# Identity matmuls in front of six waits of TensorE, in a one-core hybrid encoder step

## The chip, the core and the metric

The kernel runs on one core of one Trainium2 chip. A core has a matrix engine (TensorE, "PE" in the profile, with its weight loads shown apart as "PEld"), a vector engine (DVE), a scalar engine (ACT), GpSimd (POOL), and SyncE (SP), whose queue issues most of the DMAs. Each engine runs its own instruction stream in order; they meet only at semaphores. The metric is the time of one execution in device microseconds; lower is better.

## The reference, cut to what matters

Two layers of an encoder are run for 512 prompt tokens and 32 sample tokens, which the kernel holds side by side as 544 columns. In float32:

```python
# layer 0
qkv_a, z_a, b_a, a_a, q_b, k_b, v_b, f_b = split(rmsnorm(x, g) @ w_in)   # 1024 -> 3596 columns
oa, s_new = gated_delta_rule(qa, ka, va, g, beta, s0)    # chunks of 64 tokens, 4 heads
ob = fox_attention(qb, k_all, v_all, lf_all)             # causal, 4 heads of 128, forget bias
x = x + concat([oa, ob]) @ w_out
# layer 1
q, k, v = split(rmsnorm(x, g) @ w_in)
x = x + swa_attend(q, k, v, valid, sinks) @ w_out        # 16 query heads of 64, window 128
# both layers, after the mixer
x = x + cross_attend(rmsnorm(x, g), mk, mv, wq, wo)      # 4 heads of 128, 256 memory tokens
x = x + square(relu(rmsnorm(x, g) @ w_up)) @ w_down      # 1024 -> 4096 -> 1024
# at the end
y = rmsnorm(x, g_final)                                  # out as rows of tokens
```

The delta rule solves, per chunk of 64 tokens and head, a unit lower triangular system, and then carries a state from chunk to chunk.

## The kernel before, in words

**Projections.** Activations lie as 128 features by 544 tokens. Weights come in panels of 128 x 2048 through two buffers; ACT rounds a panel to its high part, POOL takes the low part, and every product is three matmuls (high by high, high by low, low by high) over two halves of 272 tokens (`block`, the matmul on L744). These are most of TensorE's work.

**Attentions.** There are four of them, all run by the function `attention(name)`: "fox" (17 units), "cross0" and "cross1" (10 units each) and "swa" (40 units). A unit is one block of query tokens for one or two heads. On TensorE a unit has three steps: `scores` (L828) writes the scores into `LP`; `turn` (L851) transposes the probabilities into `MP` banks 0 and 1; `values` (L877, L868 for the sample unit of fox) multiplies them with the values into `MP` bank 2 or 3. Between them DVE takes the maximum (`nm`), ACT the exponential, DVE the normalisation, and ACT copies the transposed probabilities back. The loop over `i` is a software pipeline: at `i` it issues `turn` of unit `i - lag`, `values` of unit `i - lag - 1`, `scores` of unit `i + 1`, and then `also(i)`, a hook that only fox uses. `lag` is 2 for fox and 3 for the others. So the first two score groups are issued at once, and the third one (at `i` = 1) is the first to wait for another engine: for the exponentials of the first unit in the cross attentions, for its maximum in fox and swa. In fox the hook at `i` = 0 waits for ACT's copies of the transposed keys (`turn_act`) and of the sample's forget rows (`rows_act`).

**Ahead of swa** TensorE turns keys and values into rows (L1294, L1295) and then waits until ACT has copied the last of them (`swa_copied`).

**Delta rule.** The steps are written out in one list, `DELTA`, which each engine walks. `gram` builds the decay and gram matrices of a tile, `turns` transposes the start of the inverse, `x..` and `d..` double the solved blocks, `turn_in` fills in transposes of other inputs. Tiles 0 and 1 have 128 tokens (matmuls of 64 x 64), tile `TT` is the sample (32 x 32). `inverse` issues them on L1092, `turn_in` on L1076.

**The last turns.** After the last MLP block DVE scales `x` into `yT`; TensorE waits for it (`y_scaled`), transposes it tile by tile (L1310) and, after the first tile, sums the squares of every token (L1318, ten small matmuls). ACT and DVE scale the turned rows into `y_rows`, and SP sends them out.

In the trace a plain float32 matmul is two MATMUL records, a transpose one.

Of the kernel before, what the change touches and what calls it, by code (L numbers as in the profile page):

```python
# [5 lines left out]
def build_program(nc, t):  # L6
# [29 lines left out]
    NTOK = TT + 1  # L36
# [42 lines left out]
    with ctx:  # L79
# [34 lines left out]
        ident = place("ident", [128, 128])  # L114
# [152 lines left out]
        LP = ctx.enter_context(nc.psum_tensor("LP", [128, 4, 512], f32))  # L267
        MP = ctx.enter_context(nc.psum_tensor("MP", [128, 4, 512], f32))
# [37 lines left out]
        turn_pe, turn_act = sem("turn_pe"), sem("turn_act")  # L306
# [7 lines left out]
        sum_pe, sum_act, sum_dve = sem("sum_pe"), sem("sum_act"), sem("sum_dve")  # L314
# [421 lines left out]
        def _(pe):  # L736
# [76 lines left out]

            XS = (xh, xl)

            def attention(name, also=lambda i: None):
                u0, count = GROUP[name]

                def scores(u):
                    U = UNITS[u]  # L820
                    if u >= 2:

                        pe.wait_ge(ex_ready if UNITS[u - 2]["kind"] == "cross" else nm_ready, u - 1)
                    for g, keys in enumerate(U["keys"]):
                        stacked = U["stack"] > 1
                        rows, at = (slice(NS * g, NS * g + NS), 0) if stacked else (slice(0, U["P"]), g * U["nk"])
                        for kT, n in keys:
                            mm = pe.matmul(LP[rows, score_bank(u, at // 512), at % 512:at % 512 + n], U["q"][g],  # L828
                                           kT, start=True, stop=True, skip_group_check=True)
                            at += n  # L830
                    mm.then_inc(sc_ready, 1)

                def turn(u):
                    U = UNITS[u]
                    P, G_ = U["P"], U["G"]
                    pe.wait_ge(p_ready, u + 1)
                    if U["kind"] == "swa":
                        pe.wait_ge(second_ready, u - GROUP["swa"][0] + 1)
                    if U["stack"] > 1 or u and UNITS[u - 1]["stack"] > 1:

                        pe.wait_ge(pt_ready, u)
                    elif u >= 2:

                        pe.wait_ge(pt_ready, u - 1)
                    for g in range(G_):
                        at = g * U["nk"]
                        for c, (n, _) in enumerate(U["v"]):
                            to = (c * G_ + g) * P
                            bank = (u + to // 512) % 2
                            to %= 512  # L850
                            mm = pe.transpose(MP[0:n, bank, to:to + P], probs_of(u, slice(at, at + n)),  # L851
                                              ident[0:P, 0:P])
                            at += n
                    mm.then_inc(tr_ready, 1)

                def values(u):
                    U = UNITS[u]
                    P, G_, last = U["P"], U["G"], len(U["v"]) - 1
                    pe.wait_ge(pt_ready, u + 1)
                    if u >= 2:  # L860
                        pe.wait_ge(ol_ready, u - 1)
                    if U["stack"] > 1:
                        pe.wait_ge(vpast_in, 16)
                        for g in range(U["stack"]):
                            w = P // U["stack"]
                            for c, (n, v) in enumerate(U["v"]):
                                at = c * P + g * w
                                mm = pe.matmul(MP[:, 2 + u % 2, g * w:g * w + w], v[g], U["PT"][0:n, u % 2, at:at + w],  # L868
                                               start=(g == 0 and c == 0), stop=(c == last), skip_group_check=True)
                        mm.then_inc(o_ready, 1)  # L870
                        return
                    shared = len(U["v"][0][1]) < G_
                    for g in range(1 if shared else G_):
                        w = (G_ if shared else 1) * P
                        for c, (n, v) in enumerate(U["v"]):
                            at = (c * G_ + g) * P
                            mm = pe.matmul(MP[0:U["D"], 2 + u % 2, g * P:g * P + w], v[g],  # L877
                                           U["PT"][0:n, u % 2, at:at + w], start=(c == 0), stop=(c == last),
                                           skip_group_check=True)
                    mm.then_inc(o_ready, 1)  # L880

                lag = 2 + extra_lag(name)
                for i in range(-1, count + lag + 1):
                    if lag <= i < count + lag:
                        turn(u0 + i - lag)
                    if i > lag:
                        values(u0 + i - lag - 1)
                    if i + 1 < count:
                        scores(u0 + i + 1)
                    also(i)  # L890


# [40 lines left out]
            for k in range(KT):  # L933
                for n_, (w, X) in enumerate(((wgh, xh), (wgh, xl), (wgl, xh))):
                    for half, (a, b) in enumerate(TOKENS):
                        mm = pe.matmul(MP[0:GATES, half, 0:HALF], w[:, k, :], X[:, k, a:b],
                                       start=(k == 0 and n_ == 0), stop=(k == KT - 1 and n_ == 2))
# [141 lines left out]
            def inverse(name, j):  # L1079
                _, a, P = TOK[j]  # L1080
# [4 lines left out]
                def dve_at(step_):  # L1085
                    pe.wait_ge(inv_dve[s], count_of(INV_DVE[s], step_, r))
# [10 lines left out]
                if name == "gram":  # L1097
# [18 lines left out]
                        mm = mm_(out, ua[:, H + h, cols_], ua[:, h:H + h + 1:H, cols_])  # L1116
                    mm.then_inc(inv_pe[s], 1)
                elif name == "turns":
                    dve_at("gram")
                    for h, p in each():  # L1120
                        mm = mm_(b1[p, h * C:h * C + C], TmT[s][p, h, :], ident[p, p])
                    mm.then_inc(inv_pe[s], 1)
                elif name[0] == "x":
                    k = sizes.index(int(name[1:]))
                    pe.wait_ge(inv_pool[s], r * len(sizes) + k + 1)
                    if k:
                        dve_at(f"dt{sizes[k - 1]}")
                    else:
                        act_at("turns")
                    for h, p in each():  # L1130
                        mm = mm_(b0[p, h * C:h * C + C], BT[s][p, k % 2, h, :], Tm[s][p, h, :])
                    mm.then_inc(inv_pe[s], 1)
                elif name[0] == "d":
                    k = sizes.index(int(name[1:]))
                    act_at(f"x{sizes[k]}")
                    if k:
                        dve_at(f"dtt{sizes[k - 1]}")
                    if k < len(sizes) - 1:
                        for h, p in each():
                            mm = mm_(b0[p, w + h * C:w + h * C + C], TmT[s][p, h, :], Xm[s][p, h, :])  # L1140
                        mm.then_inc(inv_pe[s], 1)
                    for h, p in each():
                        mm = mm_(b1[p, h * C:h * C + C], Xm[s][p, h, :], TmT[s][p, h, :])
                    mm.then_inc(inv_pe[s], 1)
                else:
                    dve_at(f"dtt{sizes[-1]}")
                    pe.wait_ge(turn_used, max(TURNS.index(("k", j)), TURNS.index(("v", j))) + 1)

                    for h, p in each():
                        mm_(b0[p, 128 * h:128 * h + 128], TmT[s][p, h, :], vbt[j][p, h, :])  # L1150
                    for h in range(H):
                        mm = mm_(b1[:, h * C:h * C + C], kbe[j][parts[0], h, :], TmT[s][parts[0], h, :])
                    mm.then_inc(inv_pe[s], 1)
# [136 lines left out]
            for j, a, P in TOK:  # L1290
                if j >= 2:
                    pe.wait_ge(swa_copied, 1 + j - 1)
                for c in range(2):
                    pe.transpose(MP[0:P, 2 * (j % 2), 128 * c:128 * c + 128], k_c[:, c, a:a + P], ident[:, :])  # L1294
                    mm = pe.transpose(MP[0:P, 2 * (j % 2) + 1, 128 * c:128 * c + 128], v_c[:, c, a:a + P],  # L1295
                                      ident[:, :])
                mm.then_inc(swa_turned, 1)
            pe.wait_ge(swa_copied, 1 + NTOK)
            attention("swa")
            pe.wait_ge(ol_ready, sum(GROUP["swa"]))  # L1300
# [1 line left out]

            for j, a, P in TOK:
                if j == 0:
                    pe.wait_ge(y_scaled, KT)
                if j >= 2:
                    pe.wait_ge(y_left, j - 1)
# [5 lines left out]
                if j == 0:  # L1313
# [3 lines left out]
                    for i, at, Q in TOK:  # L1317
                        mm = pe.matmul(MP[0:Q, 0, i:i + 1], acc[:, at:at + Q], ones[:, 0:1], start=True, stop=True,  # L1318
                                       skip_group_check=True)
# [1022 lines left out]
```

## Time and profile before

| what | us |
|---|---|
| median of 3 runs | 1736.03 |
| lowest, highest | 1728.38, 1737.19 |
| the profiled execution | 1740.99 |
| its span, first to last instruction | 1739.3 |
| TensorE busy | 1649.8 (95%) |
| DVE, ACT, POOL busy | 748.7, 602.7, 533.2 |

The mean granted clock of TensorE in the profiled execution is 0.963 of full speed. The row `PEclk` of the page gives it slice by slice: 9 tenths or more nearly everywhere, 8 in five of the forty slices. Windows of the trace give it for any stretch: 1.00 is the upper level (2.4 GHz), 0.50 the lower (1.2 GHz), and a value between them is a stretch with some of both.

### The profile page before, as it was taken

How to read it: one execution, taken by the hardware profiler on the slowest of the kernel's cores; microseconds unless marked ns; L12 is line 12 of the kernel's file. 1: busy time of each engine (PE TensorE's matmuls, PEld its weight loads, DVE VectorE, ACT ScalarE, POOL GpSimd, SP SyncE). 2: the span in 40 equal slices, each digit the busy share in tenths (PEclk: the TensorE clock that was granted, in tenths of full speed). 3: DMA queues.
4: the chain of work that ended last, by engine and by line, in shares of the span. 5: the costliest groups of instructions: out<-in, count | busy, mean ns of one | idle time of the engine just before them, and what ended most of it. 6: DMA issues, size and time to landing. Idle time of an engine off the chain costs nothing.

```text
span 1739.3 us, 31388 instructions
## 1 busy us (share of the span) xinstructions
PE 1649.8 (95%) x13305; PEld 1561.1 (90%) x13305; DVE 748.7 (43%) x1338; ACT 602.7 (35%) x1105; POOL 533.2 (31%) x192
## 2 busy tenths in 40 slices
PE   6999988999989999989989998999889999999998
PEld 6999967888978999989989995559878999999998
DVE  4592165435746422313224425765755322222245
ACT  5132264224434422313123216773443413222232
POOL 4633202121441333433433341003522344343341
PEclk9998999999999999999989998899999999999998
DMA  5232111004340233232212331001410332322321
GB/s 152 74 96 74 51 51 56 2 2 133 103 131 16 68 97 97 74 98 73 94 57 94 98 127 56 1 1 61 153 55 25 98 97 74 98 76 93 96 72 52
DMA packets 123051, 131.67 MB, mean 76 GB/s; under 512 B 6285, under 2 KB 115122, under 8 KB 122930
## 3 DMA queue, kind: packets, MB, share of 16 engines
q1 hardware_dynamic: 116064, 123.27, 21.9%
q10 hardware_dynamic: 6866, 6.63, 1.2%
q8 instruction: 95, 1.56, 0.4%
q14 instruction: 26, 0.21, 0.0%
HBM read 122.44 MB, written 7.45 MB: 75 GB/s over the span
## 4 chain that ended last, share of the span: by engine, by line
PE 87%; DVE 7%; ACT 3%; issue 2%; DMA 0%; ACTq 0%; DVEq 0%
PE LP L744 69%; PE LP L828 3%; PE MP L877 3%; PE LP L1092 3%; PE MP L851 2%; DVE acc L1851 1%; DVE xl L1858 1%; DVE probs L1919 1%; PE MP L1186 1%; PE MP L1172 1%; DVE nm L1924 1%; PE MP L1180 0%; DMA stage<-in_w_in_ab 0%; DVE nm L1896 0%; PE LP L1310 0%
## 5 line engine op out<-in xcount | busy, mean ns | idle before, releaser
L638 POOL TENSOR_TENSOR wl<-stage,wh 128x2048 fp32r<-128x2048 f32 x107 | 493.3, 4610 | 1013.2 <-ACT wh L1342 1013.1
L744 PE MATMUL LP<-xh,wh 128*128 128x272 f32 x2176 | 462.2, 294 | 22.9 <-issue 9.7
L744 PE MATMUL LP<-xh,wl 128*128 128x272 f32 x2176 | 455.8, 291 | 0.0
L744 PE MATMUL LP<-xl,wh 128*128 128x272 f32 x2176 | 455.1, 291 | 0.0
L744 PEld LDWEIGHTS LP<-xh,wh 128*128 128x128 f32 x2176 | 348.2, 192 | 26.5 <-DVE xl L1858 8.8
L1342 ACT CAST wh<-stage 128x2048 fp32r<-128x2048 f32 x107 | 203.7, 1905 | 460.2 <-PE LP L744 459.4
L744 PEld LDWEIGHTS LP<-xl,wh 128*128 128x128 f32 x2176 | 348.3, 192 | 2.2 <-issue 2.2
L744 PEld LDWEIGHTS LP<-xh,wl 128*128 128x128 f32 x2176 | 345.5, 192 | 0.0
L744 PE MATMUL LP<-hh,wh 128*128 128x272 f32 x1024 | 211.5, 288 | 0.0
L744 PE MATMUL LP<-hh,wl 128*128 128x272 f32 x1024 | 210.9, 288 | 0.0
L744 PE MATMUL LP<-hl,wh 128*128 128x272 f32 x1024 | 210.6, 287 | 0.0
L2242 DVE TENSOR_TENSOR hsq<-rel 128x544 f32<-128x544 f32 x64 | 70.5, 1101 | 283.7 <-ACT rel L1762 277.2
L744 PEld LDWEIGHTS LP<-hl,wh 128*128 128x128 f32 x1024 | 160.2, 188 | 0.0
L744 PEld LDWEIGHTS LP<-hh,wl 128*128 128x128 f32 x1024 | 159.6, 189 | 0.0
L744 PEld LDWEIGHTS LP<-hh,wh 128*128 128x128 f32 x1024 | 159.5, 188 | 0.0
L2257 DVE TENSOR_TENSOR dtmp<-LP,rstd 128x544 f32<-128x544 f32 x64 | 46.3, 724 | 234.8 <-PE LP L744 234.8
L1762 ACT ACTIVATE rel<-LP 128x544 f32<-128x544 f32 x64 | 40.1, 626 | 253.3 <-PE LP L744 253.3
L1851 DVE TENSOR_TENSOR acc<-acc,sq 128x544 f32<-128x544 f32 x49 | 81.9, 1671 | 23.4 <-ACT sq L1367 23.4
L1858 DVE SCALAR_TENSOR_TENSOR xl<-x,cols,xh 128x544 fp32r<-128x544 f32 x48 | 78.6, 1648 | 24.0 <-ACT xh L1372 23.8
L1367 ACT ACTIVATE sq<-x 128x544 f32<-128x544 f32 x56 | 36.8, 658 | 138.2 <-DVE x L1872 75.0
L721 POOL TENSOR_TENSOR BT<-LT,level 128x256 f32<-128x256 f32 (+1 forms) x24 | 18.1, 768 | 141.4 <-DVE LT L2142 113.0
L851 PEld LDWEIGHTS MP<-ident,probs 128*128 128x128 f32 (+2 forms) x269 | 31.1, 150 | 29.5 <-DVE probs L1950 16.4
(374 smaller groups left out, 1811.1 us busy)
## 6 DMA issues: line engine op xcount, KB each, us to landing
stage<-in_w_up SPq DMA_DIRECT2D x32, 1024.0 KB, 5.4
stage<-in_w_down SPq DMA_DIRECT2D x32, 1024.0 KB, 5.2
stage<-in_w_in_ab SPq DMA_DIRECT2D x13, 1024.0 KB, 5.2
stage<-in_w_xkv SPq DMA_DIRECT2D x8, 1024.0 KB, 5.3
stage<-in_w_in_c SPq DMA_DIRECT2D x6, 1024.0 KB, 5.0
stage<-in_w_out_ab SPq DMA_DIRECT2D x4, 1024.0 KB, 9.9
stage<-in_w_xq SPq DMA_DIRECT2D x4, 1024.0 KB, 5.5
stage<-in_w_xo SPq DMA_DIRECT2D x4, 1024.0 KB, 5.9
```

Of the source, the lines that this page charges most:

```text
L638: pool.tensor_tensor(wl[s][:, :], stage[s][:, :], wh[s][:, :].bitcast(f32), ALU.subtract).then_inc(w_lo, 1)
L744: mm = pe.matmul(LP[:, 2 * slot + half, 0:b - a], weights, X[part][:, k, a:b], start=(first and n_ == 0), stop=(last and n_ == 2), skip_gr ...
L828: mm = pe.matmul(LP[rows, score_bank(u, at // 512), at % 512:at % 512 + n], U["q"][g], kT, start=True, stop=True, skip_group_check=True)
L851: mm = pe.transpose(MP[0:n, bank, to:to + P], probs_of(u, slice(at, at + n)), ident[0:P, 0:P])
L877: mm = pe.matmul(MP[0:U["D"], 2 + u % 2, g * P:g * P + w], v[g], U["PT"][0:n, u % 2, at:at + w], start=(c == 0), stop=(c == last), skip_gr ...
L1092: return pe.matmul(out, lhsT, rhs, start=start, stop=stop, skip_group_check=True)
L1342: act.copy(wh[s][:, :], stage[s][:, :]).then_inc(w_hi, 1)
L1762: act.activation(rel[:, k % 2, :].rearrange("p (a n) -> p a n", a=2), LP[:, 2 * (k % 2):2 * (k % 2) + 2, 0:HALF], ACT.Relu).then_inc(relu_ ...
L1851: dve.tensor_tensor(acc[:, :], acc[:, :], sq[:, k % 2, :], ALU.add).then_inc(sq_used, 1)
L1858: dve.scalar_tensor_tensor(out=xl[:, k, :], in0=x[:, k, :], scalar=gain(n_, k), in1=xh[:, k, :].bitcast(f32), op0=ALU.mult, op1=ALU.subtra ...
L2242: dve.tensor_tensor(hsq[:, k % 2, :], rel[:, k % 2, :], rel[:, k % 2, :], ALU.mult).then_inc(hsq_ready, 1)
L2257: dve.tensor_tensor(two(dtmp[:, k % 2, :]), banks(k), two(rstd[:, :]), ALU.mult).then_inc(drained, 1)
```

## The change: what it does

A helper `keep_busy(count, bank)` issues `count` matmuls of the 128 x 128 float32 identity with itself into a PSUM bank. Nobody reads what they write, and they signal no semaphore. It is called

- in every attention, at `i` = 0, after the scores of the second unit and before the hook: 8 matmuls in fox and swa, 16 in each cross attention, into `MP` bank 2 (in fox behind an added wait for the eleventh copy of turned rows, which frees the bank);
- in the delta rule, ahead of the first `turns` step (tile 0 only, it runs once): 6, into `MP` bank 1, behind an added wait for ACT's reading of the gate sums there;
- between the turned keys and values and the wait ahead of swa: 6, into `LP` bank 3;
- ahead of the wait for `yT` at the end: 8, into `MP` bank 2.

That is 68 matmuls in an execution. No other engine's stream changes.

```diff
--- before.py
+++ after.py
@@ -813,6 +813,11 @@
 
             XS = (xh, xl)
 
+            def keep_busy(count, bank):
+
+                for _ in range(count):
+                    pe.matmul(bank[:, 0:128], ident[:, :], ident[:, :], start=True, stop=True, skip_group_check=True)
+
             def attention(name, also=lambda i: None):
                 u0, count = GROUP[name]
 
@@ -887,6 +892,10 @@
                         values(u0 + i - lag - 1)
                     if i + 1 < count:
                         scores(u0 + i + 1)
+                    if i == 0:
+                        if name == "fox":
+                            pe.wait_ge(turn_act, 2 * NTOK + 1)
+                        keep_busy({"fox": 8, "swa": 8}.get(name, 16), MP[:, 2, :])
                     also(i)
 
 
@@ -1116,6 +1125,9 @@
                         mm = mm_(out, ua[:, H + h, cols_], ua[:, h:H + h + 1:H, cols_])
                     mm.then_inc(inv_pe[s], 1)
                 elif name == "turns":
+                    if j == 0:
+                        pe.wait_ge(sum_act, 1)
+                        keep_busy(6, MP[:, 1, :])
                     dve_at("gram")
                     for h, p in each():
                         mm = mm_(b1[p, h * C:h * C + C], TmT[s][p, h, :], ident[p, p])
@@ -1295,6 +1307,7 @@
                     mm = pe.transpose(MP[0:P, 2 * (j % 2) + 1, 128 * c:128 * c + 128], v_c[:, c, a:a + P],
                                       ident[:, :])
                 mm.then_inc(swa_turned, 1)
+            keep_busy(6, LP[:, 3, :])
             pe.wait_ge(swa_copied, 1 + NTOK)
             attention("swa")
             pe.wait_ge(ol_ready, sum(GROUP["swa"]))
@@ -1302,6 +1315,7 @@
 
             for j, a, P in TOK:
                 if j == 0:
+                    keep_busy(8, MP[:, 2, :])
                     pe.wait_ge(y_scaled, KT)
                 if j >= 2:
                     pe.wait_ge(y_left, j - 1)
```

Where they stand, by TensorE's stream. The rows give the line, the operation, the output and the inputs, the shape, and the semaphores waited for; the new helper stands ahead of the later code, so that the lines of the kernel after are higher (L828 is L833 there, L1092 is L1101).

Start of cross0, before: the last projection matmul, the scores of units 0 and 1, of units 2 and 3, and the first transposes.

```order
L744 MATMUL LP<-xh,wl_57 128x272 x2
L828 MATMUL LP<-kvT,q_x 128x256 [waits nm_ready,drained,rstd_ready]
L828 MATMUL LP<-kvT,q_x 128x256
L828 MATMUL LP<-kvT,q_x 128x256 [waits nm_ready]
L828 MATMUL LP<-kvT,q_x 128x256
L828 MATMUL LP<-kvT,q_x 128x256 [waits ex_ready]
L828 MATMUL LP<-kvT,q_x 128x256
L828 MATMUL LP<-kvT,q_x 128x256 [waits ex_ready]
L828 MATMUL LP<-kvT,q_x 128x256
```

The same place after.

```order
L744 MATMUL LP<-xh,wl_57 128x272 x2
L833 MATMUL LP<-kvT,q_x 128x256 [waits nm_ready,drained,rstd_ready]
L833 MATMUL LP<-kvT,q_x 128x256
L833 MATMUL LP<-kvT,q_x 128x256 [waits nm_ready]
L833 MATMUL LP<-kvT,q_x 128x256
L819 MATMUL MP<-ident 128x128 x16
L833 MATMUL LP<-kvT,q_x 128x256 [waits ex_ready]
L833 MATMUL LP<-kvT,q_x 128x256
L833 MATMUL LP<-kvT,q_x 128x256 [waits ex_ready]
L833 MATMUL LP<-kvT,q_x 128x256
```

The sixteen stand between the second unit's scores and the first wait for `ex_ready`, with no wait of their own.

Start of swa after: the last turned rows (`k_c`, `v_c`), the six, the scores of units 0 and 1, the eight, the scores of units 2 and 3. Before, the rows of L819 are not there and the others are the same.

```order
L1306 MATMUL MP<-ident,k_c 32x128
L1307 MATMUL MP<-ident,v_c 32x128
L819 MATMUL LP<-ident 128x128 x6
L833 MATMUL LP<-k_c,q_c 128x128 [waits ex_ready,swa_copied]
L833 MATMUL LP<-k_c,q_c 128x128
L833 MATMUL LP<-k_c,q_c 128x256 [waits ex_ready]
L833 MATMUL LP<-k_c,q_c 128x256
L819 MATMUL MP<-ident 128x128 x8
L833 MATMUL LP<-k_c,q_c 128x256 [waits nm_ready]
L833 MATMUL LP<-k_c,q_c 128x256
```

Both groups come ahead of a wait: of `swa_copied` the first, of `nm_ready` the second.

The delta rule after: the last matmuls of `gram` for the sample tile, the transposes of tile 0's keys, the six, and `turns` of tiles 0, 1 and the sample (`TmT_128`, `TmT_129`, `TmT_130`).

```order
L1101 MATMUL MP<-ua 32x2x32 x4
L1085 MATMUL MP<-ident,ua 128x128 x4
L819 MATMUL MP<-ident 128x128 [waits sum_act]
L819 MATMUL MP<-ident 128x128 x5
L1101 MATMUL LP<-ident,TmT_128 64x64 [waits inv_dve0]
L1101 MATMUL LP<-ident,TmT_128 64x64 x7
L1101 MATMUL LP<-ident,TmT_129 64x64 [waits inv_dve1]
L1101 MATMUL LP<-ident,TmT_129 64x64 x7
L1101 MATMUL MP<-ident,TmT_130 32x32 [waits inv_dve2]
L1101 MATMUL MP<-ident,TmT_130 32x32 x3
```

The six stand ahead of the turns of tile 0, two waits earlier than the wait for the sample's `TmT`.

## Rows read from the trace of the kernel before

**Rows 1.** The page: TensorE's busy time, its granted clock by slice.

```profile
PE 1649.8 (95%) x13305; PEld 1561.1 (90%) x13305; DVE 748.7 (43%) x1338; ACT 602.7 (35%) x1105; POOL 533.2 (31%) x192
...
PEclk9998999999999999999989998899999999999998
```

**Rows 2.** Windows: stretch, length, busy of five engines, clock, DMA share, GB/s.

```profile
222.74:225.52 2.78, 0.00 (x0) 0.00 (x1) 1.00 (x5) 1.10 (x5) 0.00 (x0) 1.00 1.05 405
...
237.94:244.77 6.83, 6.83 (x25) 5.81 (x26) 2.18 (x8) 3.44 (x8) 0.00 (x0) 0.50 0.00 0
...
285.73:292.56 6.83, 6.20 (x80) 5.15 (x82) 3.46 (x6) 1.16 (x4) 1.85 (x3) 0.50 0.01 2
514.41:517.84 3.43, 0.00 (x1) 0.00 (x0) 3.43 (x1) 0.00 (x0) 3.43 (x1) 1.00 0.00 0
517.84:524.66 6.82, 5.44 (x14) 3.58 (x15) 3.87 (x13) 3.66 (x14) 0.25 (x1) 0.50 0.47 154
...
1057.14:1074.21 17.07, 16.05 (x47) 9.26 (x47) 10.27 (x45) 11.15 (x42) 0.00 (x0) 0.50 0.14 49
...
1282.43:1289.25 6.82, 4.30 (x12) 3.22 (x12) 4.07 (x9) 2.95 (x12) 1.39 (x1) 0.50 0.49 154
...
1726.15:1732.98 6.83, 6.83 (x34) 6.54 (x33) 2.25 (x3) 2.76 (x7) 0.00 (x0) 0.50 0.32 131
1732.98:1734.27 1.29, 1.27 (x12) 0.91 (x10) 0.75 (x1) 0.69 (x1) 0.00 (x0) 1.00 0.84 321
```

**Rows 3.** Chain of waits, cross0: start, length, what; eight 128x128 float32 records.

```profile
525.87 0.89 PE MP L877 x8
```

**Rows 4.** Timeline of TensorE, both cross attentions: start, length, what, idle before.

```profile
512.44 1.97 PE L828 MATMUL LP<-kvT,q_x 128*128 128x256 f32 x8 [0.86 <-issue]
519.22 3.78 PE L828 MATMUL LP<-kvT,q_x 128*128 128x256 f32 x8 [4.81 <-ACT probs L1395]
...
1284.95 3.78 PE L828 MATMUL LP<-kvT,q_x 128*128 128x256 f32 x8 [4.81 <-ACT probs L1395]
```

**Rows 5.** Timeline, delta rule: turns of tiles 0, 1; DVE; turns of TT; three doublings.

```profile
281.65 1.47 PE L1092 MATMUL LP<-ident,TmT 64*64 64x64 f32 x32
...
283.32 1.79 DVE L2146 TENSOR_TENSOR TmT<-chunk_ident,TmT 32x128 f32<-32x128 f32 x1
...
285.16 0.43 PE L1092 MATMUL MP<-ident,TmT 32*32 32x32 f32 x8 [2.04 <-DVE TmT L2146]
...
287.40 1.97 PE L1092 MATMUL LP<-Tm,BT 64*64 64x64 f32 x32
...
294.81 1.15 PE L1092 MATMUL LP<-Tm,BT 64*64 64x64 f32 x32
...
300.01 1.15 PE L1092 MATMUL LP<-Tm,BT 64*64 64x64 f32 x32
```

**Rows 6.** Timeline of TensorE, swa: first scores, then the sample unit's in three groups.

```profile
1054.20 1.57 PE L828 MATMUL LP<-k_c,q_c 64*128 64x128 f32 x8 [1.63 <-ACT v_cn L1806]
1056.14 1.13 PE L828 MATMUL LP<-k_c,q_c 64*128 64x256 f32 x4 [0.36 <-DVE nm L1929]
...
1078.04 0.40 PE L828 MATMUL LP<-kcT,q_c 64*32 64x128 f32 x2
...
1090.03 0.40 PE L828 MATMUL LP<-kcT,q_c 64*32 64x128 f32 x2
...
1104.80 0.40 PE L828 MATMUL LP<-kcT,q_c 64*32 64x128 f32 x2
```

**Rows 7.** Window in swa, between the second and third of those groups.

```profile
1091.28:1098.10 6.82, 6.61 (x19) 3.85 (x20) 4.02 (x20) 5.75 (x23) 0.00 (x0) 0.50 0.00 0
```

**Rows 8.** Timeline of TensorE, last turns: the first tile, then the sums of squares.

```profile
1725.27 1.17 PE L1310 MATMUL LP<-ident,yT 128*128 128x128 f32 x8 [2.12 <-DVE yT L2270]
1726.23 2.01 PE L1318 MATMUL MP<-ones,acc 128*128 128x1 f32 x10
```

**Rows 9.** Window in the last turns.

```profile
1731.00:1732.00 1.00, 1.00 (x7) 1.00 (x6) 0.02 (x1) 0.03 (x1) 0.00 (x0) 0.50 1.00 406
```

## The prediction, made before the changed kernel was run

> **What bounds the kernel now.** I read the page first. TensorE is busy for 95% of the span, and the clock row stays at 8 or 9 tenths in every slice [rows 1]. So the projections fill the kernel; the change touches none of them and can act only in the short stages where TensorE waits. Then I cut the stages into windows, with the clock beside the busy time. TensorE's clock has two levels here, 1.00 and 0.50 of full speed (2.4 and 1.2 GHz). In both cross attentions, in the delta rule and in the last turns it falls after the engine has stood still for a few microseconds, and it comes back after TensorE has worked for a while at the lower level [rows 2]. Last I read the timeline around each fall, to see which engine is waited for there.
>
> The change removes nothing. It fills waits of TensorE with matmuls whose result is thrown away. It gains only if three things hold: the clock would have fallen, it now does not, and TensorE is what the stage waits for in the stretch saved.
>
> **Price of the filler.** Eight records of the 128x128 float32 matmul take 0.89 us in a row at full clock [rows 3], 0.111 us each, and a matmul is two records: 0.22 us. Sixteen are 3.6 us, eight 1.8 us, six 1.3 us; all 68 are 15 us at full clock. No other engine does more. What of the 15 us lies in front of work that could have started is the cost.
>
> **Price of the lower clock.** A stretch that is TensorE's alone costs half its length. Two repeated patterns show what it costs in the real stages. In swa the same five units take 11.99 us from group to group at full clock (1078.04 to 1090.03) and 14.77 us when 6.82 us of them lie at the lower clock (1090.03 to 1104.80) [rows 6, 7]: 2.78 / 6.82 = 0.41 us per microsecond. In the delta rule one doubling takes 5.20 us at full clock (294.81 to 300.01) and 7.41 us (287.40 to 294.81) when 5.16 us of it are low [rows 5, 2]: 0.43. I use 0.42.
>
> **Cross attentions.** TensorE stands still for 4.81 us in each, waiting for ACT's exponentials of the first unit [rows 4]; DVE is the late one behind that, busy all through the wait [rows 2]. The sixteen matmuls take 3.6 of the 4.81 us and end 1.2 us before TensorE is needed, so they delay nothing. If that cover shrank below 3.6 us, they would cost the difference. With them TensorE is idle for 1.2 us, and I expect no fall. What is saved is 5.44 and 4.30 us of busy time at the lower clock [rows 2]: 9.74 x 0.42 = 4.1 us. I take off 0.4 us, because right after the gap the third and fourth units' scores (3.78 us for eight records, low) come out at the pace at which DVE can take them. Term 3.7 us, bounds 2.8 (DVE decides until the first transposes) and 4.9 (all of it at one half).
>
> **Fox.** Idle 2.78 us and no fall: the clock is 1.00 in the gap and falls only at 237.94, 15 us later [rows 2]. There, between 234 and 240, TensorE runs narrow matmuls of the sample unit, which the filler does not touch. The eight (1.8 us) fit into 2.78, and the added wait for ACT's eleventh copy is over by then: that copy precedes the key copies, which ACT makes ahead of what ends the gap. In this execution the term is 0. A fall after a gap of 2.04 us in the delta rule and none after 2.78 us here tells me that falls are not tied to the length of the gap alone, and that other executions may have one here. Term 0.5 us, bounds -0.3 and +1.7 (four low microseconds avoided).
>
> **Delta rule.** The six stand ahead of the turns of tiles 0 and 1, which today wait for nothing. They push these back by 1.3 us, but behind them TensorE stands still for 2.04 us, since DVE takes 1.79 us for the sample's `TmT` [rows 5], which the change leaves where it is. So the push is absorbed. If that slow DVE step ran in some 0.3 us instead, the six would cost the whole 1.3 us. The clock was low from 285.73 to 292.56, 6.83 us, 6.20 busy [rows 2]. Avoiding all of it is worth 6.20 x 0.42 = 2.6 us. But the filler lies ahead of busy work and not in the gap: the 2.04 us shrink to 0.7 us, a short matmul follows, then a further wait, so the clock may fall a little later all the same. I take somewhat under half: 1.2 us, bounds -1.3 and +2.6.
>
> **Swa.** The first six fill 1.3 of a gap of 1.63 us [rows 6] and cost nothing. The eight stand ahead of the third unit's scores, which waited for 0.36 us only [rows 6]: 1.8 - 0.36 = 1.4 us too late. The fourth unit's scores wait for DVE again and run at full clock in place of low, so about 0.6 us reach DVE. The low stretch is long, 1057.14 to 1074.21, 17.07 us [rows 2], but the filler ends before its first third: at its start the scores are 64 rows deep and wait on DVE, and the stage later falls to the lower clock with no idle time of a microsecond before it, as at 1091.28 [rows 7]. So I expect the fall to come later, not to stay away: some 3 us of TensorE's work less at the lower clock, 1.3 us, less 0.6. Term 0.6 us, bounds -1.4 (the fall where it was) and +6.4 (16.05 busy microseconds x 0.42, less 0.4).
>
> **Last turns.** The eight (1.8 us) fit into 2.12 us of waiting [rows 8]. Low from 1726.15 to 1732.98 [rows 2]. At full clock the ten sums of squares (2.01 us) are between 1.0 and 2.01 us, which brings the first evicted tile up to 1.0 us forward; the later transposes gain more, but the output DMAs then run at 406 GB/s with a share of 1.00 [rows 9], so little of it reaches the end. Term 1.0 us, bounds 0 and 2.7.
>
> A rule of the skill speaks against this term. The Trainium skill, page "TensorE: Matmul & The Clock Gate", Part 4 (PE-mode transpose), says that transposes do not count as activity for the clock as matmuls do. By that rule the clock falls in the last turns anyway, soon after the filler, the term is 0 and the sum 6.0 us. The trace disagrees: after the sums of squares at 1728.2 TensorE ran transposes only, and the clock rose during them, at 1732.98 [rows 2].
>
> **Sum.** 3.7 + 0.5 + 1.2 + 0.6 + 1.0 = 7.0 us. Against the profiled execution's own 1740.99 us that is 1734.0. That execution is 5.0 us above the median of the three runs, 1736.03, so the forecast for the median is 1729.0 us. With all lower bounds the sum is -0.2 us, with all upper ones 18.3 us; both ends at once are unlikely.
>
> **The rivals.**
>
> *The clock stays up through the start of swa too.* For it: 1054.20 to 1057 had only short waits, and the fall comes at their end [rows 6, 2], so 14 matmuls more may carry the engine over the fill of the pipeline. Against it: stretches without fillers in the same stage fall as well [rows 7]. It would replace swa's 0.6 by some 5.5 us, and the delta rule's 1.2 by 2.6: 13.3 us, 1722.7 us.
>
> *The fillers do not hold the clock.* The fall only moves behind them, into the same work. For it: the lower level in fox came without an idle gap, from narrow matmuls alone [rows 2]. Against it: the fall in cross0 follows 3.43 us of complete idleness [rows 2]. Then half the cross term stays, the delta rule and swa give 0 or less: 1.9 - 0.3 + 0.5 = 2.1 us, 1733.9 us.
>
> *Slower.* Place: the eight in swa. They delay the third unit by 1.4 us, and the fall of the clock moves from the fill of the pipeline, where DVE decides, into the part where TensorE decides. If two more low stretches of the length of rows 7 come up in swa (2 x 2.78 us), the 1.4 us reach the end, the delta rule's 1.3 us are uncovered, and the rest brings 0, that is 8.3 us slower, 1744.3 us. It decides only if the cross attentions, whose fillers lie wholly in idle time, give nothing at the same time; with their 3.7 us it is 4.6 us slower, 1740.6 us. Against it: twice 4.81 us of idle time [rows 4] are too plain.
>
> **How the numbers follow.** Forecast (1729.0) 0.52; clock up in swa too (1722.7) 0.22; not held (1733.9) 0.18; slower (1740 and above) 0.08. A measurement of this kernel can tell about 0.5% from no change, 8.7 us: faster means below 1727.3, slower above 1744.7. The three runs before spread over 8.8 us by themselves, so a median of three may lie 3 us off. The forecast case is then below 1727.3 in a third of its cases (0.17), the swa case in nearly all (0.20): 0.37. The slower case gets there in half of its cases, with 0.02 from the spread: 0.06. Within 0.5%: 0.57. The range of 8 in 10 goes from 1719.5 to 1738.0; it leaves out the far end of the swa case and most of the slower one. The likeliest case alone spans 1724 to 1734.
>
> **What would show it.** In the profile after: no row at 0.50 in the first 6 us after the scores of the second unit in either cross attention, and a wait of about 1.2 us instead of 4.81 before the third unit's scores; the first eight score records after it in about 2 us and not 3.78. In the delta rule the wait for `TmT` near 0.7 us. In swa the third unit's scores right behind the filler and a low stretch that starts later than 3 us after the first scores. At the end 1.00 during the ten sums. The forecast is wrong if the clock is at 0.50 in a cross attention, if its third unit comes more than 4.9 us after the second, or if swa, first scores to projection, changes by more than 4 us.

## The result, and the profile after

The kernel after takes 1711.22 us (median of 4 runs, 1710.72 to 1726.52), the kernel before 1736.61 us (4 runs, 1728.38 to 1739.32). The ratio is 0.9862 with a 95% interval of 0.9824 to 0.9899: 1.4% faster, some 25 us, where I had forecast 7. The time lies outside my range of 1719.5 to 1738.0. Here and below, means and medians leave out the few executions that are more than 1.5% above the fastest of the same kernel.

The first rows of the page of the kernel after, which answer to [rows 1]:

```profile
span 1709.0 us, 31660 instructions
...
PE 1635.6 (96%) x13441; PEld 1554.6 (91%) x13441; DVE 747.8 (44%) x1338; ACT 602.7 (35%) x1105; POOL 533.2 (31%) x192
...
PEclk9998999998999999999999999899999999999999
```

TensorE issues 136 more matmul records (68 fillers of two records) and is busy for 14 us less: the others ran at a higher clock. The span is 30.3 us shorter, 1739.3 to 1709.0; that is more than the medians differ by, since the profiled execution before is a long one (1740.99). To find where, I cut both traces at the same instructions. In brackets stands how much of the stage lay at the lower clock.

| stage, on TensorE | before, us | after, us | difference |
|---|---|---|---|
| forget sums to fox | 77.63 (9.7) | 77.90 (10.2) | +0.27 |
| fox, from its third scores | 46.50 (6.8) | 46.50 (6.8) | 0.00 |
| delta rule, from `turns` of the sample | 109.77 (13.7) | 107.01 (7.2) | -2.76 |
| cross0, from its third scores | 24.55 (5.4) | 22.75 (0.0) | -1.80 |
| **cross0's output, first MLP, in_c** | **505.35 (20.5)** | **487.72 (0.0)** | **-17.63** |
| swa | 115.61 (41.0) | 111.21 (23.9) | -4.40 |
| out1, memory, xq1 | 108.36 (3.4) | 106.89 (0.0) | -1.47 |
| cross1, from its third scores | 24.02 (4.3) | 22.75 (0.0) | -1.27 |
| second MLP | 416.30 (3.4) | 415.93 (0.0) | -0.37 |
| last turns | 14.00 (9.7) | 12.69 (2.3) | -1.31 |

(At the very start the kernel after is 0.6 us late, by its first inputs.) More than half of the gain comes from a stage with no filler in it. The two windows of that stage, of the kernel before and of the kernel after:

```profile
543.77:1049.12 505.35, 490.86 (x3848) 488.94 (x3848) 160.03 (x188) 137.42 (x140) 179.50 (x39) 0.98 0.27 87
```

```profile
539.93:1027.65 487.72, 482.89 (x3849) 481.59 (x3849) 160.04 (x188) 137.52 (x140) 179.64 (x39) 1.00 0.28 89
```

Idle time of TensorE (length less the first busy number) goes from 14.49 to 4.83 us, 9.7 us less, and its busy time falls by 8.0 us for the same instructions, which is the clock. What ended the idle time stands in the waits of TensorE between 560 and 1040 us, before and after (us in total, times, longest):

```profile
PE LP L744 <- issue: 9.7, 4, 4.1
PE LP L744 <- DVE xl L1858: 2.1, 2, 1.8
PE LP L744 <- DVEq L1874: 1.9, 1, 1.9
```

```profile
PE LP L744 <- DVE xl L1872: 2.1, 2, 1.8
PE LP L744 <- DVEq L1888: 1.9, 1, 1.9
```

The first row is gone: 9.7 us in which TensorE waited for no engine. Its four places in the timeline before:

```profile
770.94 0.81 PE L744 MATMUL LP<-xh,wh 128*128 128x272 f32 x2 [3.65 <-issue]
...
773.73 0.39 PE L744 MATMUL LP<-xh,wh 128*128 128x272 f32 x1 [0.85 <-issue]
...
874.56 0.82 PE L744 MATMUL LP<-xh,wh 128*128 128x272 f32 x2 [4.07 <-issue]
...
877.63 0.39 PE L744 MATMUL LP<-xh,wh 128*128 128x272 f32 x1 [1.12 <-issue]
```

They are 104 us apart, one turn of the first MLP's loop, at its start. (The loop has three turns, so the program jumps back twice.) The clock falls in each of the two long waits:

```profile
770.42:777.25 6.83, 5.46 (x23) 5.37 (x24) 0.00 (x0) 0.00 (x0) 3.38 (x1) 0.50 0.32 90
...
872.82:883.06 10.24, 7.38 (x32) 7.29 (x33) 0.00 (x0) 0.00 (x0) 4.21 (x1) 0.50 0.33 105
```

These are 17.1 of the 20.5 us at the lower clock. The other 3.4 us, at 575.86, come long before the first jump; profiles without a filler in cross0 have them even where no jump waits, and there they cost some 0.3 us (below). The DMA view names what else happens there: the queue that brings instructions. Between 770 and 1020 us, before and after (packets, MB, share):

```profile
q8 instruction: 19, 0.31, 0.6%
```

```profile
q8 instruction: 3, 0.05, 0.1%
```

A packet is 16 KB. Between 755 and 955 us the contrast is plainer: 17 packets of this queue before, and after none at all, only one of another queue:

```profile
q8 instruction: 17, 0.28, 0.7%
```

```profile
q14 instruction: 1, 0.01, 0.0%
```

The view does not name the engine that the packets are for, but their spacing points to TensorE: inside a turn of the kernel before they come 13 to 18 us apart, and 128 matmuls with their 128 weight loads, 256 instructions, take 16.0 us at the 0.125 us of one matmul. So before, TensorE's code of the loop is fetched again in every turn, and the jump back waits for it. After, it is not. The Trainium skill, page "Runtime: NRT & Kernel Launch", section "Instruction fetch mechanics", says that code comes in blocks of 16 KB or 256 instructions, and that TensorE's instruction memory has 128 KB, 2048 instructions, which is eight blocks. It also says that a taken jump waits for a fetch when its target is outside the present window; it calls that window two pages, which is the memory that it gives for the other engines. The packet size agrees. A window of two blocks for TensorE does not: after, the loop jumps back over more than six blocks without a packet. By that page, an estimate: the loop has 768 matmuls and as many weight loads, six blocks and some more, so it lies in seven blocks or in eight depending on where it begins. How many blocks TensorE holds, and why one place is fetched anew and another not, no run here shows.

Where the fillers stand, the picture is as forecast. Cross0 after: the sixteen matmuls, and the third and fourth scores, at full clock.

```profile
512.18 3.73 PE L819 MATMUL MP<-ident 128*128 128x128 f32 x32
517.18 2.04 PE L833 MATMUL LP<-kvT,q_x 128*128 128x256 f32 x8 [1.27 <-ACT probs L1409]
```

The wait is 1.27 us in place of 4.81, and the eight score records take 2.04 us in place of 3.78 [rows 4]. In the delta rule the six, and the wait for the sample's `TmT`, 1.03 us against 2.04 [rows 5] (I had forecast 0.7):

```profile
282.34 1.50 PE L819 MATMUL MP<-ident 128*128 128x128 f32 x12
...
285.95 0.43 PE L1101 MATMUL MP<-ident,TmT 32*32 32x32 f32 x8 [1.03 <-DVE TmT L2160]
```

And in the last turns the eight, the first tile and the ten sums, 1.18 us against 2.01 [rows 8]:

```profile
1694.03 1.95 PE L819 MATMUL MP<-ident 128*128 128x128 f32 x16
...
1696.30 1.09 PE L1324 MATMUL LP<-ident,yT 128*128 128x128 f32 x8 [0.33 <-DVE yT L2284]
...
1697.23 1.18 PE L1332 MATMUL MP<-ones,acc 128*128 128x1 f32 x10
```

### The profile page after: what moved, and what is told of

It reads as the page before. It is cut to its first block, busy times and chain, and to the rows that moved or that the text cites. A ratio compares the mean times of both kernels' runs of the same rounds, so it can differ in the third digit from the quotient of the medians.

```text
span 1709.0 us, 31660 instructions
## 1 busy us (share of the span) xinstructions
PE 1635.6 (96%) x13441; PEld 1554.6 (91%) x13441; DVE 747.8 (44%) x1338; ACT 602.7 (35%) x1105; POOL 533.2 (31%) x192
## 4 chain that ended last, share of the span: by engine, by line
issue 42%; PE 42%; POOL 8%; DVE 4%; ACT 2%; DMA 1%; ACTq 0%; POOLq 0%; DVEq 0%
PE LP L744 34%; POOL wl L638 8%; PE LP L1101 2%; DVE acc L1865 1%; PE MP L882 1%; PE LP L833 1%; DVE xl L1872 1%; DMA stage<-in_w_in_ab 1%; PE MP L856 0%; DVE conv_sum L2022 0%; DMA stage<-in_w_xkv 0%; PE MP L945 0%; ACT sq L1381 0%; PE MP L873 0%; PE MP L1101 0%
## 5 line engine op out<-in xcount | busy, mean ns | idle before, releaser
L744 PE MATMUL LP<-xh,wh 128*128 128x272 f32 x2176 | 457.3, 291 | 15.3 <-DVE xl L1872 8.1
L744 PEld LDWEIGHTS LP<-xh,wh 128*128 128x128 f32 x2176 | 344.5, 190 | 20.4 <-DVE xl L1872 10.7
L744 PEld LDWEIGHTS LP<-xl,wh 128*128 128x128 f32 x2176 | 344.2, 190 | 0.0
L744 PEld LDWEIGHTS LP<-xh,wl 128*128 128x128 f32 x2176 | 341.8, 190 | 0.0
```

Of the source, the lines that this page charges most:

```text
L744: mm = pe.matmul(LP[:, 2 * slot + half, 0:b - a], weights, X[part][:, k, a:b], start=(first and n_ == 0), stop=(last and n_ == 2), skip_gr ...
```

## The experiments

Two theories. *Place*: most of the gain is that the added instructions shift the first MLP's loop in TensorE's code, so that it is not fetched anew. *Clock*: the gain is what the fillers do to the clock. The runs vary shift and activity apart from each other. A small matmul of a 32 x 32 corner has the same four instructions as a filler (two matmuls, two weight loads) and takes about 0.07 us at a filler's place and 0.11 to 0.12 us at the start of the program.

### The same instructions, little activity

```diff
-                    pe.matmul(bank[:, 0:128], ident[:, :], ident[:, :], start=True, ...)
+                    pe.matmul(bank[0:32, 0:32], ident[0:32, 0:32], ident[0:32, 0:32], start=True, ...)
```

> Every filler stays where it is, with the same number of instructions, but multiplies a 32 x 32 corner of the identity instead of all of it, so that the array does almost nothing. Place theory (most of the gain is that TensorE's loop of the first MLP lies elsewhere in its code and is no longer fetched again in every turn): no idle time put down to issue between 700 and 900 us, 3 instruction packets and not 19 between 770 and 1020 us, and about 17 us of the 25 us stay: 1719 us. Clock theory (the gain is the clock that the fillers hold up): both cross attentions fall to 0.50 again as before, and the time is that of before, 1736 us.

1719.46 us (median of 10, 1712.45 to 1736.02), ratio 0.9893 (0.9854 to 0.9933). The instruction packets are 3 and no wait for issue is left in the loop, yet cross0 is as before (24.44 us, 5.3 of it low):

```profile
513.25 1.19 PE L819 MATMUL MP<-ident 32*32 32x32 f32 x32
518.13 2.50 PE L834 MATMUL LP<-kvT,q_x 128*128 128x256 f32 x5 [3.69 <-ACT probs L1410]
```

The place theory holds. What is missing is the clock's part: 8 us to the 1711 of the first measurement, or 5 us by the two ratios (0.9893 and 0.9862), since the kernel before was slower in this job (1738.98).

### Only the fillers behind the first MLP

```diff
-                        if name == "fox":
-                            pe.wait_ge(turn_act, 2 * NTOK + 1)
-                        keep_busy({"fox": 8, "swa": 8}.get(name, 16), MP[:, 2, :])
+                        keep_busy({"fox": 0, "cross0": 0, "swa": 8, "cross1": 16}[name], MP[:, 2, :])
...
-                    if j == 0:
-                        pe.wait_ge(sum_act, 1)
-                        keep_busy(6, MP[:, 1, :])
```

> Only the fillers behind the first MLP stay: swa (6 and 8), cross1 (16), last turns (8). Fox, delta rule and cross0 are as before. Place theory: TensorE's code up to and with the loop of the first MLP lies as before, so the two idle times of 3.7 and 4.1 us put down to issue come back at the turns of the loop, and 19 instruction packets between 770 and 1020 us; the time is 1736 less the direct worth of these fillers, about 4 us: 1732. Clock theory: no such idle times are tied to the code, swa gives most of it, 1721 us.

1729.28 us (10 runs), ratio 0.9947 (0.9914 to 0.9980). The waits for issue are back in the first MLP, at another time of the execution and in the same place of the program. TensorE's waits between 560 and 1040 us, and the instruction queue between 770 and 1020:

```profile
PE LP L744 <- issue: 9.9, 4, 3.9
```

```profile
q8 instruction: 21, 0.34, 0.6%
```

### Only the fillers ahead of the first MLP, and only those of the cross attentions

```diff
-            keep_busy(6, LP[:, 3, :])
...
-                    keep_busy(8, MP[:, 2, :])
...
-                        keep_busy({"fox": 8, "swa": 8}.get(name, 16), MP[:, 2, :])
+                        keep_busy({"fox": 8, "cross0": 16, "swa": 0, "cross1": 0}[name], MP[:, 2, :])
```

> Only the fillers ahead of the first MLP stay: fox (8), delta rule (6), cross0 (16). Place theory: the first MLP's loop lies as in the kernel after, no idle time of issue there, 17 us plus 4 us for these fillers: 1715 us. Clock theory: half of the gain at most, 1724 us or more, and idle times of issue in the loop as before.

> Only the two cross attentions keep their sixteen. Their direct worth by my prediction is 3.7 us. Ahead of the first MLP this is 64 instructions more than before, against 122 in the kernel after. Place theory: a step at some number of instructions, so either no idle times of issue in the first MLP (1716 us) or both (1732 us), nothing between. Clock theory: 1732 us, whatever the loop does.

The second kernel keeps `keep_busy(16, ...)` in the two cross attentions and drops every other call. 1713.20 us (0.9875, 0.9808 to 0.9942) and 1714.73 us (0.9880, 0.9815 to 0.9945), 4 runs each, against 1738.98 for the kernel before in the same job. Neither has a wait for issue; both have 3 packets. Sixteen matmuls in each cross attention bring nearly all of the gain, but most of it by where they put the loop: the thirty-two are worth only some 3 to 4 us by their work (below). In the first of them cross1, which has no filler, takes 24.54 us, and cross0, which has one, 22.76.

### The kernel after, shifted back by a block

```diff
             pe.wait_ge(mask_done, FIRST_MASKS)
+            for _ in range(34):
+                pe.matmul(LP[0:32, 3, 0:32], ident[0:32, 0:32], ident[0:32, 0:32], start=True, stop=True, ...)
             pe.wait_ge(par_loaded, 16 * 8)
```

> The kernel after, with 34 matmuls of a 32 x 32 corner (136 instructions) at the very start of TensorE's program, where it waits 10 us for inputs anyway. The first MLP's loop then lies 258 instructions later in the code than in the kernel before, one fetch block of 256 and two more. Place theory: same place within a block as before, so the idle times of issue in the loop and the 19 instruction packets come back: about 1729 us, 18 more than after. Clock theory: all fillers are there, 1711 us.

1730.94 us (10 runs), ratio 0.9984 (0.9953 to 1.0014): with all fillers in, most of the gain is gone. The same two views:

```profile
PE LP L744 <- issue: 9.1, 4, 4.1
```

```profile
q8 instruction: 21, 0.34, 0.6%
```

This is the plainest single run: 34 matmuls in ten microseconds in which TensorE has nothing to do cost 16 to 20 us more than seven hundred microseconds later.

### The kernel before, with 16, 64 and 30 small matmuls at its start

The edit is that of the last run, in the kernel before, with another count: no filler at any wait.

> The kernel before with 16 such small matmuls (64 instructions) at the very start and no filler anywhere: nothing that could hold the clock up at a wait. Place theory: the loop lies as in the run with the cross fillers alone, so no idle times of issue and 3 packets; 1719 to 1722 us. Clock theory: 1738 us, as before.

> The kernel before with 64 small matmuls (256 instructions) at the start. Place theory, if the place counts only within a block of 256 instructions: idle times of issue as before, 1738 us. If it is the absolute place or the sheer number of instructions that counts, they are gone, 1720 us. Clock theory: 1738 us.

> The kernel before with 30 small matmuls (120 instructions) at the very start, no filler at any wait. Both MLP loops then lie where the kernel after and the run with the late fillers had theirs without idle times of issue. Place theory: no such idle time in either loop (3 and about 5 instruction packets in the two windows), 1720 us, the same as with the 32 x 32 fillers in the places of the change. Clock theory: 1735 us.

*Sixteen*: 1733.94 us (9 runs, and one more of 3809.53), ratio 0.9995 (0.9956 to 1.0035). Both theories' sentences miss in part; for the total the clock theory's 1738 was the nearer number. The first MLP is free of the waits, as the place theory says (489.22 us). But the second MLP has them now. Instruction packets between 770 and 1020 and between 1450 and 1720, and two rows of the timeline there:

```profile
q8 instruction: 3, 0.05, 0.1%
```

```profile
q8 instruction: 22, 0.36, 0.6%
```

```profile
1515.61 0.81 PE L744 MATMUL LP<-xh,wh 128*128 128x272 f32 x2 [3.90 <-issue]
...
1619.29 0.81 PE L744 MATMUL LP<-xh,wh 128*128 128x272 f32 x2 [4.07 <-issue]
```

The second MLP takes 432.63 us in place of 416.30. I had looked at one loop; there are two of the same length at different places. That is an explanation found afterwards; the run with thirty, chosen so that both loops should be free, is its test.

*Sixty-four*, 256 instructions: 1741.29 us (10 runs), ratio 1.0022 (0.9982 to 1.0062), waits for issue of 9.5 us in the first MLP, 18 packets. A shift by one block changes nothing, as does, in the run before, 258 beyond the old place.

*Thirty*, 120 instructions: 1728.80 us (12 runs, 1713.11 to 1737.42), ratio 0.9950 (0.9912 to 0.9988). No wait for issue in either loop, 3 and 5 instruction packets, and the stage with the first MLP takes 488.05 us; so far as expected. The total missed my 1720 by 9 us. Swa is the reason in the profiled execution: 126.53 us, 68.3 low, against 115.61 and 41.0 before. There is no filler in it; the clock alone does that:

```profile
1034.79:1161.32 126.53, 119.01 (x480) 69.57 (x481) 84.81 (x360) 87.15 (x328) 0.62 (x1) 0.73 0.03 10
```

Over all runs, the first MLP's loop was fetched anew at shifts of 0, 256 and 258 instructions, and not at 64, 120 to 122 and 162; the second's at 64, and not at 0, 26, 120 to 122, 128 and 242 (modulo 256 for the second; each added wait is counted as one instruction, which no trace shows).

### After again, and two attempts at more

> The kernel after, unchanged, beside the others on the same chip. Its distance to the kernel before with 30 small matmuls is the clock's part alone, with the place of both loops good in both: by the difference to the run with the 32 x 32 fillers 8 us; by my prediction's terms 7 us. If both parts are as thought: 1711 us.

1714.94 us (6 runs, 1713.55 to 1727.31), ratio 0.9862 (0.9811 to 0.9913): the same ratio as the first time. The profiled execution is a long one, 1727.31 us, yet the stage with the first MLP is as short in it (487.71 us); the delta rule (116.01) and swa (114.55) make the difference.

```diff
             def forget_sums():
 
+                keep_busy(10, MP[:, 3, :])
                 pe.wait_ge(gate_dve, GATE_LOGF)
```

> The kernel after with ten more fillers of the full size in the one long wait that it leaves, 2.56 us before the forget sums at 143 us, where the clock falls for 10 us in both profiles. Clock part: up to 10.2 x 0.42 = 4.3 us less, 1707 us; if the small matmuls of the sums behind it let the clock fall all the same, 1711 us. Place part: the first MLP's loop moves by 40 instructions more, 162 in all; if it leaves the good range there, 1729 us.

1718.83 us (9 runs), ratio 0.9902 (0.9867 to 0.9937). The stage from the forget sums to fox fell from 77.90 to 74.89 us, 3.0 of the 4.3 us hoped for. No better than after in total: swa took 127.15 us there, 64.9 low.

```diff
-            keep_busy(6, LP[:, 3, :])
...
-                        keep_busy({"fox": 8, "swa": 8}.get(name, 16), MP[:, 2, :])
+                        keep_busy({"fox": 8, "swa": 0}.get(name, 16), MP[:, 2, :])
+                    if name == "swa" and i % 5 == 3:
+                        keep_busy(3, LP[:, 3, :])
```

> As after, but swa's own fillers (6 and 8) are taken out and 3 stand behind every sample unit's scores instead, eight times, where TensorE waits 0.7 us for DVE. The clock fell near that place in every profile, in single head pairs; 24 to 68 us of swa were low. If it holds there: swa 111 to 127 us becomes some 101 us, and the kernel 1701 us with little spread. If the low rows of swa come from the depth of 64 rows everywhere, 1711 us and the old spread. The second MLP's loop moves to 280 instructions beyond before, 24 within a block, which was good in two runs.

1707.58 us (6 runs, 1701.16 to 1712.31), ratio 0.9810 (0.9756 to 0.9863), the fastest kernel of the study, 7 us below after in the same job. Swa falls to 103.55 us and stays at full clock from 1052 on:

```profile
1042.00:1052.00 10.00, 9.30 (x32) 6.16 (x32) 7.54 (x32) 6.59 (x26) 0.00 (x0) 0.51 0.32 105
1052.00:1135.50 83.50, 81.42 (x456) 52.19 (x456) 71.68 (x306) 72.81 (x280) 0.00 (x0) 1.00 0.00 1
```

The low stretch at the fill of the pipeline, which the change's own fillers stand in, is there without them: 10 us of it. The profiled execution took 1710.92 us, no less than that of the kernel after (1710.72), although swa was 7.7 us shorter: the delta rule took 114.38 us in place of 107.01, low for 25 us, as in three others (29 us), two with its filler and one without.

### The two causes apart

Mean of the runs of five kernels, with their number and the standard error of the mean:

| | no full-size fillers | all fillers of the change |
|---|---|---|
| first loop fetched anew | 1736.2 (66 runs, 0.8) | 1732.9 (10, 1.5) |
| neither loop fetched anew | 1724.6 (22, 1.7) | 1716.5 (10, 2.0) |

The place is worth 11.6 us without fillers and 16.4 with them (standard errors 1.9 and 2.5), the fillers 3.3 and 8.1 us (1.7 and 2.6). That each is worth more beside the other is not clear of this noise. (First column: the kernel before; the 32 x 32 fillers and the thirty small matmuls. Second: the shift by 34; after, twice.) The cells mix jobs, and the cell of 22 mixes two kernels that differ: against the kernel before in its own job, the 32 x 32 fillers gain 16.9 us and the thirty small matmuls 8.0. Within one job, after is 9.2 us below the thirty small matmuls, and after shifted by 34 is 2.2 us below before. The stage itself is the better witness of the place. From cross0's output projection to swa's first scores it takes 508.3 to 510.4 us in the four profiles in which the first loop is fetched anew, and 492.8 to 494.3 in the nine others.

## Why the prediction was wrong

**The step that failed** is in the first paragraph: "So the projections fill the kernel; the change touches none of them and can act only in the short stages where TensorE waits." It can act on every loop behind it, through the place of the loop in the code. That made 17.6 of the 30.3 us between the two profiled executions: 9.7 us of idle time and 8.0 us of clock, nearly all of which the idle time had cost. All my cases were about the clock, so no case held it, and no size in my sum could make up for it: with all upper bounds together, 18.3 us, the forecast is 1717.7, still 6.5 us above the 1711.22 measured. The row was there, in the page of the kernel before:

```profile
L744 PE MATMUL LP<-xh,wh 128*128 128x272 f32 x2176 | 462.2, 294 | 22.9 <-issue 9.7
```

And the clock fell at 770.42 and 872.82 us in the middle of the projections, with no other engine waited for. I read only the stages in which the fillers stand.

**The sum of the clock terms**, 7.0 us, lies between the 3.3 and the 8.1 us measured for the fillers by themselves, which are known to some 2 and 3 us. (In swa's term, 1.3 less 0.6 is 0.7 and not 0.6, and its upper bound 6.3 and not 6.4; nothing hangs on it.)

- *Price of the filler.* 3.73 us for sixteen, forecast 3.6. Right.
- *Price of the lower clock.* Cross0 lost 1.80 us for 5.4 low, 0.33 per microsecond, cross1 1.27 for 4.3, 0.30. I had taken 0.42 from swa and the delta rule and then 0.4 us off: too much for the fill of a pipeline.
- *Cross attentions*, 3.7 us: measured 1.80 + 1.27 = 3.1 in the two stages. The mechanism was right: in seven profiles with the filler cross0 took 22.75 or 22.76 us, in six without it 24.09 to 24.56; cross1 22.75 to 22.77 with it and 23.56 to 24.54 without. At full clock the fourth unit's transposes wait for DVE for 0.6 us. Some 0.3 us each come on top in the MLPs behind: without the filler the clock falls once more for 3.4 us, 48 to 58 us after the first fall (575.86 and 1330.21 before), and the second MLP then takes 416.2 to 416.3 us in place of 415.9 in most profiles. So the whole is close to the forecast.
- *Fox*, 0.5: measured 0.0 in this pair, as the profiled execution alone had said. The other part, that other executions may have a fall in the gap, came true: it fell at 225.3 and 225.5 us, for 3.4 us, in two of the seven profiles without the filler (the late fillers alone, and the thirty small matmuls), and in none of the six with it. In the first of them fox then took 47.24 us from its third scores, 0.7 more.
- *Delta rule*, 1.2: the fall at 285.73 did not come, and one doubling took 5.21 us at once. From the sample's turns to the third doubling it took 12.19 us in three profiles with the filler and 13.52 to 13.62 in the other three, and without it 14.66 to 14.88 in five and 13.58 and 13.62 in two. So the filler brings some 1 to 2.7 us at this place in most executions. The stage as a whole is no witness: 106.45 us without a filler (the run with sixty-four), 116.01 us with it (after again). In the pair 2.66 of its 2.76 us come up to the third doubling; further on the fall at 319.86 us stayed away too, and another came at 385.71. What the filler does that far behind it stays open.
- *Swa*, 0.6: 4.40 us in the pair of profiles, and again no witness. With these fillers it took 111.21, 112.13, 114.55, 114.59 and 127.15 us, without full-size ones 111.09, 111.45, 111.85, 115.61, 115.96, 126.52 and 126.53. The third unit's scores came right behind the filler, as forecast, and the fall came at 8.3 us after the first scores in place of 2.9. Nothing of it is seen in the length of the stage. I had named a change of swa by more than 4 us as a sign that the forecast is wrong; the pair shows 4.40, but by these lengths the sign was badly chosen, as swa moves by more than that without any change to it.
- *Last turns*, 1.0: 14.00 to 12.69 us here. The term was at the low end: over all profiles the turns took 11.30 or 11.31 us with the filler in five of six (12.69 is the sixth), and 12.31 to 14.29 in the seven without it, so 1.0 to 3.0 us. The clock stayed at 1.00 until the work ended at 1704, though TensorE ran only transposes from 1698.35 on. That speaks again for the rows, and against what the Trainium skill says on its page "TensorE: Matmul & The Clock Gate", Part 4 (PE-mode transpose), that transposes do not count as matmuls do.

**The rivals.** Slower: nothing of it. Not held: in the cross attentions it was held in every profile. Clock up in swa too: it was not, and its 13 us would have been the nearest number for the wrong reason.

**What stays open** is why swa and the delta rule differ by up to 16 and 10 us between executions of kernels that issue the same work there. Profiles show the low stretches, not why they come in one execution and stay out in the next. That spread is at least part of why 4 to 12 runs of one kernel span 10 to 25 us: the two profiles of the kernel after, 15.8 us apart, differ by 9.0 us in the delta rule and 3.3 us in swa.

## What to carry to other kernels

Adding instructions to an engine changes where its later loops lie in the code. Before a gain or a loss is put down to what the instructions do, look at idle time with "issue" as its releaser at the start of a loop's turns, and at the instruction queue's packets during the loop; a run with the same number of instructions and no work tells the two apart. A filler pays where an engine stands idle for long in front of work that only it decides, as in the cross attentions; where a stage swings by itself, its length in one pair of profiles proves nothing; a short piece of it, compared over many profiles, can.

## What the runs showed that I had not expected

- A loop that is fetched anew costs 14 to 18 us here over three turns, nearly half of it through the clock: 9.1 to 9.9 us of idle time in five of the thirteen profiles and none in the others, by a shift of 0 to 258 instructions ahead of it.
- Two loops of the same code can be good and bad independently: a shift by 64 instructions cured the first and spoiled the second, for no gain at all.
- TensorE's matmuls of 64 rows run with falls of the clock although the engine is busy for 92% of the stage (106.70 of 115.61 us before); with three full matmuls in a wait of 0.7 us, eight times in the stage, it stayed up for 83 us in the one profile of that kernel, whose six runs are also the fastest of the study.
